# Odd attention of a two-block diffusion model on one core: one activation for both sinks, and one turned tile in four copied by VectorE

## The chip, the core and the metric

The kernel runs on one core of a Trainium2 chip. The metric is the device time of one execution in microseconds. The kernel before took 2181.8 us, the median of 3 runs (2180.72 to 2182.32).

## What is computed

The reference is two transformer blocks in fp32, one after the other, on 256 tokens of width 1024 (`first_block` and `second_block`). The change touches only the attention of the second block's odd layer, `window_attention`: 16 query heads in groups of four on 4 key heads of width 64, 256 latent tokens that see the latent keys at a distance of at most 128 and all 256 context keys, and one sink logit a head that takes part in the softmax and has no value:

```python
s_loc = einsum(q, k) * scale            # banded: |i-j| <= 128, else -inf
s_ctx = einsum(q, k_c) * scale
m = max(max(s_loc), max(s_ctx), s_sink)
e_loc, e_ctx = exp(s_loc - m), exp(s_ctx - m)
denom = sum(e_loc) + sum(e_ctx) + exp(s_sink - m)
o = (e_loc @ v + e_ctx @ v_c) / denom
```

## The kernel before, in words

Every engine has its own program, written out by hand, and engines wait for each other's named events: `done` adds to an engine's output semaphore and books the event's name, and the other side waits for the count at that name. `link` makes an engine wait for its own last instruction before it goes on, and `own` for an earlier event of its own. The weights come in 1 MB chunks through a ring of three buffers. ScalarE makes the high part of each chunk (L1519, `whi`) and VectorE the rest (L2056, `wlo`), and TensorE multiplies both parts (L629 to L631, or L635 and L639 in the feed-forward phases). The phases follow each other; the odd layer (`odd` in each engine's program) lies between the MLP phase M0 and the last MLP phase M1.

The odd attention has 16 steps `s`. Step `s` treats the two query heads (`e` = 0, 1) of pair `p = s // 2` for one half of the queries, 128 of them (`qt = s % 2`). The 512 keys (256 latent, 256 context) are the columns of a PSUM bank. `R` is banks 0 to 3 and `Y` is banks 4 to 7 of `banks`. Buffers that depend on `s % 2` come twice. What happens to step `s`:

- TensorE, `scores(s)`: q x k of both heads into two banks of `R` (L1404), and the window's mask added by a matmul (L1407).
- VectorE, `maxima(s)`: the row maximum of both heads in one reduction of 1024 columns (L2824), then the negative maximum with the sink taken in, `stat[o + 2:o + 4]` (L2826), event `odmax`.
- ScalarE, `exps(s)`: the exponentials with row sums (L1954, twice), then the exponential of each sink (L1957, twice), event `odexp`. This event also frees the two banks of `R` for `scores(s + 2)`.
- VectorE, `normalise(s)`: sums (L2832), reciprocal (L2833), the two products (L2835, twice), event `odprob`.
- TensorE, `turn(s)`: eight 128x128 transposes (L903), four of head 0 into bank `Y[:, 2]` and four of head 1 into `Y[:, 3]`, with one event each, `odpt`. Each bank must have been emptied of step `s - 1`.
- ScalarE, `take(s)`: one 128x512 copy a head out of these banks into `pt` (L1966).
- TensorE, `values(s)`: the probabilities times the values (L1429), event `odpv`; after an odd `s` ScalarE's `take_o` (L1971) takes the pair's result.

The order that each engine goes through is written out as a loop: TensorE `scores(s + 2)`, four products of the last query chunk if `s < 4`, `turn(s)`, `values(s - 1)`, and at `s = 5` the rotation's matmuls `rot(5)` (L1365). VectorE `maxima(s + 1)`, `normalise(s)`, in steps 2 and 3 half a weight chunk (L2056), and at `s = 6` `rotate(5)`, the rotary embedding of the last query heads (L2583 to L2585). ScalarE `exps(s + 1)`, `take(s)`, and `take_o` in even steps from 2 on. Before the loop VectorE does `maxima(0)` and `rotate(4)`. Behind it the kernel casts the attention's result (L1988, L2258) and multiplies it with the output weights (`odo`).

Of the kernel before, what the change touches and what calls it, by code (L numbers as in the profile page):

```python
# [19 lines left out]
ALU = mybir.AluOpType  # L20
ACT = mybir.ActivationFunctionType
AX_X = mybir.AxisListType.X

P = 128
# [97 lines left out]
def program(nc, A, out_ap, book):  # L122
    ctx = ExitStack()
    with ctx:
# [97 lines left out]
        def ec(name, k=0, n=None):  # L222
            a, w = ecol_at[name]
            return ecol[:, a + k:a + k + (w - k if n is None else n)]
# [389 lines left out]
        def _(pe):  # L614
# [732 lines left out]
            def odd():  # L1347
# [62 lines left out]
                def turn(s):  # L1410
                    pe.wait_ge(dve_out.sem, dve_out.at(("odprob", s)))
                    for e in range(2):
                        if s >= 1:
                            pe.wait_ge(drained.sem, drained.at(("odpt", s - 1, e)))
                        for kt in range(4):
                            last = transpose(Y[:, 2 + e, kt * P:(kt + 1) * P], O["p"][s % 2][:, e, kt * P:(kt + 1) * P])
                        last.then_inc(pe_out.sem, pe_out.next(("odpt", s, e)))

                def values(s):
                    p, qt = s // 2, s % 2  # L1420
                    pe.wait_ge(drained.sem, drained.at(("odpt", s, 1)))
                    if qt == 0 and p == 0:
                        pe.wait_ge(dve_out.sem, dve_out.at(("odrope", 4)))
                    if qt == 0 and p >= 1:
                        pe.wait_ge(drained.sem, drained.at(("odo", p - 1)))
                    at = (p % 2) * T + qt * P
                    for kt in range(4):
                        for e in range(2):
                            last = mm(Y[64 * e:64 * e + 64, 0, at:at + P], O["vtok"][:, kt, 64 * (p // 2):64 * (p // 2) + 64],  # L1429
                                      O["pt"][s % 2][:, kt, e * P:(e + 1) * P], start=kt == 0, stop=kt == 3, skip_group_check=True)  # L1430
                    last.then_inc(pe_out.sem, pe_out.next(("odpv", s)))
# [64 lines left out]
        def _(act):  # L1496
# [10 lines left out]
            def done(ins, key):  # L1507
                ins.then_inc(act_out.sem, act_out.next(key))
# [405 lines left out]
            def odd():  # L1914
# [35 lines left out]
                def exps(s):  # L1950
                    o = 20 * (s % 2)
                    act.wait_ge(dve_out.sem, dve_out.at(("odmax", s)))
                    for e in range(2):
                        f(O["p"][s % 2][:, e, :], R[:, 2 * (s % 2) + e, :], ACT.Exp, scale=SCALE,  # L1954
                          bias=stat[:, o + 2 + e:o + 3 + e], accum_out=stat[:, o + 6 + e:o + 7 + e])
                    for e in range(2):
                        last = f(stat[:, o + 8 + e:o + 9 + e], ec("sink", 2 * (s // 2) + e, 1), ACT.Exp, scale=-1.0,  # L1957
                                 bias=stat[:, o + 2 + e:o + 3 + e])
                    done(last, ("odexp", s))

                def take(s):
                    for e in range(2):
                        act.wait_ge(pe_out.sem, pe_out.at(("odpt", s, e)))
                        if s >= 2 and e == 0:
                            act.wait_ge(pe_out.sem, pe_out.at(("odpv", s - 2)))
                        nc.scalar.copy(O["pt"][s % 2][:, :, e * P:(e + 1) * P], Y[:, 2 + e, :].rearrange("p (a q) -> p a q", a=4)) \  # L1966
                            .then_inc(drained.sem, drained.next(("odpt", s, e)))
# [65 lines left out]
        def _(dve):  # L2033
# [9 lines left out]
            def done(ins, key):  # L2043
                ins.then_inc(dve_out.sem, dve_out.next(key))

            def own(key):
                dve.wait_ge(dve_out.sem, dve_out.at(key))
# [738 lines left out]
            def odd():  # L2786
# [32 lines left out]
                def maxima(s):  # L2819
                    o = 20 * (s % 2)  # L2820
                    p, qt = s // 2, s % 2
                    dve.wait_ge(pe_out.sem, pe_out.at(("ods", s)))
                    scores = R[:, 2 * (s % 2):2 * (s % 2) + 2, :]
                    link(v.tensor_reduce(stat[:, o:o + 2], scores, AX_X, ALU.max))  # L2824

                    done(v.scalar_tensor_tensor(out=stat[:, o + 2:o + 4], in0=stat[:, o:o + 2], scalar=-SCALE, in1=ec("sink", 2 * p, 2),  # L2826
                                                op0=ALU.mult, op1=ALU.min), ("odmax", s))

                def normalise(s):
                    o = 20 * (s % 2)  # L2830
# [4 lines left out]
                        last = v.tensor_scalar(O["p"][s % 2][:, e, :], O["p"][s % 2][:, e, :], stat[:, o + 12 + e:o + 13 + e], None, ALU.mult)  # L2835
                    done(last, ("odprob", s))

                maxima(0)
                rotate(4)
                for s in range(16):  # L2840
                    if s + 1 < 16:
                        maxima(s + 1)
                    normalise(s)
                    if s in (2, 3):
                        conv(n + 7, (s - 2,))
                    if s == 6:
                        rotate(5)
                split_lo("odo", src=O["q"])
                alpha(resx)
                n = first["odo"]  # L2850
# [116 lines left out]
```

## Time and profile before

| what | value |
|---|---|
| median of 3 runs | 2181.8 us |
| lowest and highest | 2180.72, 2182.32 us |
| profiled execution, its own time | 2183.51 us |
| profiled execution, span | 2181.7 us, 33428 instructions |
| TensorE, VectorE, ScalarE busy | 97%, 81%, 54% of the span |
| HBM traffic | 503.29 MB read, 231 GB/s over the span |
| the odd attention's 16 steps | about 1888 to 1952 us |

The span is the time from the first to the last instruction on the core; the execution's own time is 1.8 us more. Busy time counts an engine's instructions alone, without waits, branches and DMA issues. The durations below are those of this one execution.

### The profile page before, as it was taken

Reading aid. Unit: us, or ns where it says so; the run is one execution under the profiler, and the core shown is the slowest. Engines: PE = TensorE matmul, PEld = TensorE weight load, DVE = VectorE, ACT = ScalarE, POOL = GpSimd, SP = SyncE. Lnnn points to the kernel's source line nnn. Section 1 sums busy time; section 2 is a strip of 40 time slices with the busy share of each in tenths; the row PEclk is TensorE's granted clock in tenths of the full one; section 3 lists DMA queues with packets and bytes.
Section 4 is the critical chain, followed back from the end, with each engine's and each line's share of the span. In section 5 each row is a group of like instructions: output and inputs, shape, how many; then the busy total and the mean of one; then the engine's idle time right before and its main releaser. Section 6 shows DMA issues by size and latency. Waiting matters only on the chain.

```text
span 2181.7 us, 33428 instructions
## 1 busy us (share of the span) xinstructions
PE 2120.3 (97%) x13811; PEld 1857.7 (85%) x13820; DVE 1777.2 (81%) x2350; ACT 1175.9 (54%) x1759; POOL 109.5 (5%) x157
## 2 busy tenths in 40 slices
PE   7999999999999999999999999999999999999997
PEld 4888888888888888898888989988888888778886
DVE  4888787788878878977888877898998998777764
ACT  3555556555455445565553544547646744575742
POOL 1000000000000000000000000000000000000000
PEclk9999999999999999999999999999999999999999
DMA  9889675478868877655888747738878877315662
GB/s 331 288 274 317 219 245 193 155 252 282 312 196 276 281 272 234 228 188 171 278 276 286 235 161 223 244 126 291 281 268 292 295 255 248 117 35 160 212 212 78
DMA packets 331024, 506.51 MB, mean 232 GB/s; under 512 B 12392, under 2 KB 239943, under 8 KB 330872
## 3 DMA queue, kind: packets, MB, share of 16 engines
q1 hardware_dynamic: 288647, 342.01, 47.7%
q0 software_dynamic: 41616, 160.44, 21.3%
q8 instruction: 109, 1.79, 0.3%
q10 hardware_dynamic: 608, 1.92, 0.3%
q14 instruction: 44, 0.35, 0.0%
HBM read 503.29 MB, written 1.05 MB: 231 GB/s over the span
## 4 chain that ended last, share of the span: by engine, by line
PE 89%; DVE 7%; DMA 2%; ACT 1%; issue 1%; POOL 0%; DVEq 0%; POOLq 0%
PE banks L635 38%; PE banks L639 19%; PE banks L629 7%; PE banks L631 6%; PE banks L630 6%; DMA plain_xs<-in_ada_w_dram 1%; PE banks L841 1%; PE banks L903 1%; PE banks L736 1%; PE banks L738 1%; PE banks L737 1%; DVE wlo L2056 1%; PE banks L1404 1%; DVE nraw L2334 1%; DMA stage<-in_ffn_wg_dram 1%
## 5 line engine op out<-in xcount | busy, mean ns | idle before, releaser
L2056 DVE TENSOR_TENSOR wlo<-stage,whi 128x1024 fp32r<-128x1024 f32 x644 | 758.3, 1219 | 124.4 <-ACT whi L1519 123.3
L1519 ACT CAST whi<-stage 128x1024 fp32r<-128x1024 f32 x644 | 643.8, 1052 | 336.5 <-PE banks L639 257.9
L635 PE MATMUL banks<-xs,whi 128*128 128x512 f32 x2176 | 688.1, 398 | 13.6 <-DVE xs L2338 9.5
L639 PEld LDWEIGHTS banks<-xs,wlo 128*128 128x128 f32 x2176 | 409.9, 188 | 97.0
L639 PE MATMUL banks<-xs,wlo 128*128 128x256 f32 x2176 | 428.6, 278 | 0.0
L629 PE MATMUL banks<-xs,whi 128*128 128x256 f32 x1216 | 351.1, 289 | 10.4 <-DVE xs L2338 5.6
L635 PEld LDWEIGHTS banks<-xs,whi 128*128 128x128 f32 x2176 | 332.2, 189 | 18.7 <-DVE xs L2338 7.6
L630 PE MATMUL banks<-xs,whi 128*128 128x256 f32 x1216 | 343.9, 283 | 0.0
L631 PE MATMUL banks<-xs,wlo 128*128 128x256 f32 x1216 | 343.9, 283 | 0.0
L635 PE MATMUL banks<-hidden_arena,whi 128*128 128x512 f32 x992 | 311.8, 395 | 0.0
L2081 DVE SCALAR_TENSOR_TENSOR arena<-modw,cact,arena 128x1024 f32<-128x1024 f32 x217 | 277.9, 1280 | 10.5 <-DMA modw<-in_w_mod_dram 6.7
L629 PEld LDWEIGHTS banks<-xs,whi 128*128 128x128 f32 x1216 | 232.9, 192 | 20.5 <-issue 8.9
L630 PEld LDWEIGHTS banks<-xs,whi 128*128 128x128 f32 x1216 | 233.0, 192 | 0.6 <-issue 0.2
L631 PEld LDWEIGHTS banks<-xs,wlo 128*128 128x128 f32 x1216 | 233.0, 192 | 0.0
L639 PEld LDWEIGHTS banks<-hidden_arena,wlo 128*128 128x128 f32 x992 | 186.5, 188 | 42.6
L639 PE MATMUL banks<-hidden_arena,wlo 128*128 128x256 f32 x992 | 195.8, 279 | 0.0
L635 PEld LDWEIGHTS banks<-hidden_arena,whi 128*128 128x128 f32 x992 | 150.1, 188 | 0.4
L610 POOL DMA_DIRECT2D modw<-in_w_mod_dram x80 | 57.1, 714 | 1125.8 <-DVE arena L2081 944.4
L635 PE MATMUL banks<-hs,whi 128*128 128x512 f32 x336 | 105.6, 395 | 0.3 <-issue 0.3
L1539 ACT COPY hid<-banks 128x512 f32<-128x512 f32 x44 | 26.0, 590 | 112.9 <-PE banks L639 112.9
L610 POOL DMA_DIRECT2D modw<-in_ada_w_dram x64 | 45.7, 714 | 753.6 <-DVE arena L2081 668.6
L1535 ACT COPY hid<-banks 128x512 f32<-128x512 f32 x44 | 26.0, 590 | 105.6 <-PE banks L639 105.6
(442 smaller groups left out, 2620.7 us busy)
## 6 DMA issues: line engine op xcount, KB each, us to landing
stage<-in_mlp_w_dram SPq DMA_DIRECT2D x96, 1024.0 KB, 5.4
modw<-in_w_mod_dram POOLq DMA_DIRECT2D x80, 1024.0 KB, 6.0
modw<-in_ada_w_dram POOLq DMA_DIRECT2D x66, 1024.0 KB, 5.5
stage<-in_ffn_wg_dram SPq DMA_DIRECT2D x44, 1024.0 KB, 5.5
stage<-in_ffn_wu_dram SPq DMA_DIRECT2D x44, 1024.0 KB, 7.4
stage<-in_ffn_wd_dram SPq DMA_DIRECT2D x44, 1024.0 KB, 7.4
stage<-in_ev_w_in_dram SPq DMA_DIRECT2D x24, 1024.0 KB, 5.9
stage<-in_w_in_dram SPq DMA_DIRECT2D x18, 1024.0 KB, 5.4
```

The source lines that it names most:

```text
L610: pool.dma_start(modw[:, c % 2, :].rearrange("p (a b) -> p a b", a=2), src).then_inc(mod_landed[c % 2], 16)
L629: mm(out, hi, xh, start=first_mm, stop=False, skip_group_check=True)
L630: mm(out, hi, xl, start=False, stop=False, skip_group_check=True)
L631: return mm(out, lo, xh, start=False, stop=last_mm, skip_group_check=True)
L635: return mm(out, whi[:, s, w:w + P], pair.rearrange("p a t -> p (a t)"), start=first_mm, stop=False, skip_group_check=True)
L639: return mm(out[:, 0:T], wlo[:, s, w:w + P], pair[:, 0, :], start=False, stop=last_mm, skip_group_check=True)
L736: mm(out, xh, hi, start=k == 0, stop=False, skip_group_check=True)
L1519: nc.scalar.copy(halves(whi[:, s, :], n, h, True), halves(stage[:, s, :], n, h)).then_inc(hi_done, 1)
L1535: done(nc.scalar.copy(hid[:, j % 2, :, :], R[:, 0:2, T:2 * T]), ("gate", name, j))
L1539: done(nc.scalar.copy(hid[:, 2, :, :], R[:, 2:4, T:2 * T]), ("up", name, j - 1))
L2056: last = v.tensor_tensor(halves(wlo[:, s, :], n, h, True), halves(stage[:, s, :], n, h), halves(whi[:, s, :], n, h, True).bitcast(F32), AL ...
L2081: v.scalar_tensor_tensor(out=acc, in0=w, scalar=cc, in1=acc, op0=ALU.mult, op1=ALU.add).then_inc(mod_step, 1)
```

## The change

Three things are altered, in the odd attention alone.

1. VectorE computes the sinks' shifted exponents itself: after `maxima` it waits for its own `odmax` and subtracts the stored sinks from the negative maxima (2 columns, `stat[o + 14:o + 16]`), event `odsink`. ScalarE waits for it and takes one exponential of both columns in place of two of one column each.
2. In odd steps ScalarE's `take` copies only head 0's turned tile. VectorE copies head 1's in `take_second(s)`, which stands between `maxima` and `normalise` of the step that follows, and after the loop for step 15. It signals on a semaphore of its own, `drained_v`.
3. TensorE waits for that semaphore where the tile of an odd step is read (`values`) or overwritten (`turn`). ScalarE in odd steps from 3 on waits for the turn of two steps before, since it no longer takes that step's last tile itself.

```diff
--- before.py
+++ after.py
@@ -1410,7 +1410,9 @@
                 def turn(s):
                     pe.wait_ge(dve_out.sem, dve_out.at(("odprob", s)))
                     for e in range(2):
-                        if s >= 1:
+                        if s >= 1 and e == 1 and s % 2 == 0:
+                            pe.wait_ge(drained_v.sem, drained_v.at(("odpt", s - 1, 1)))
+                        elif s >= 1:
                             pe.wait_ge(drained.sem, drained.at(("odpt", s - 1, e)))
                         for kt in range(4):
                             last = transpose(Y[:, 2 + e, kt * P:(kt + 1) * P], O["p"][s % 2][:, e, kt * P:(kt + 1) * P])
@@ -1418,7 +1420,11 @@
 
                 def values(s):
                     p, qt = s // 2, s % 2
-                    pe.wait_ge(drained.sem, drained.at(("odpt", s, 1)))
+                    if qt == 0:
+                        pe.wait_ge(drained.sem, drained.at(("odpt", s, 1)))
+                    else:
+                        pe.wait_ge(drained.sem, drained.at(("odpt", s, 0)))
+                        pe.wait_ge(drained_v.sem, drained_v.at(("odpt", s, 1)))
                     if qt == 0 and p == 0:
                         pe.wait_ge(dve_out.sem, dve_out.at(("odrope", 4)))
                     if qt == 0 and p >= 1:
@@ -1950,16 +1956,16 @@
                 def exps(s):
                     o = 20 * (s % 2)
                     act.wait_ge(dve_out.sem, dve_out.at(("odmax", s)))
+                    if s >= 2 and s % 2 == 1:
+                        act.wait_ge(pe_out.sem, pe_out.at(("odpt", s - 2, 1)))
                     for e in range(2):
                         f(O["p"][s % 2][:, e, :], R[:, 2 * (s % 2) + e, :], ACT.Exp, scale=SCALE,
                           bias=stat[:, o + 2 + e:o + 3 + e], accum_out=stat[:, o + 6 + e:o + 7 + e])
-                    for e in range(2):
-                        last = f(stat[:, o + 8 + e:o + 9 + e], ec("sink", 2 * (s // 2) + e, 1), ACT.Exp, scale=-1.0,
-                                 bias=stat[:, o + 2 + e:o + 3 + e])
-                    done(last, ("odexp", s))
+                    act.wait_ge(dve_out.sem, dve_out.at(("odsink", s)))
+                    done(f(stat[:, o + 8:o + 10], stat[:, o + 14:o + 16], ACT.Exp), ("odexp", s))
 
                 def take(s):
-                    for e in range(2):
+                    for e in range(2 - s % 2):
                         act.wait_ge(pe_out.sem, pe_out.at(("odpt", s, e)))
                         if s >= 2 and e == 0:
                             act.wait_ge(pe_out.sem, pe_out.at(("odpv", s - 2)))
@@ -2825,6 +2831,8 @@
 
                     done(v.scalar_tensor_tensor(out=stat[:, o + 2:o + 4], in0=stat[:, o:o + 2], scalar=-SCALE, in1=ec("sink", 2 * p, 2),
                                                 op0=ALU.mult, op1=ALU.min), ("odmax", s))
+                    own(("odmax", s))
+                    done(v.tensor_tensor(stat[:, o + 14:o + 16], stat[:, o + 2:o + 4], ec("sink", 2 * p, 2), ALU.subtract), ("odsink", s))
 
                 def normalise(s):
                     o = 20 * (s % 2)
@@ -2835,16 +2843,26 @@
                         last = v.tensor_scalar(O["p"][s % 2][:, e, :], O["p"][s % 2][:, e, :], stat[:, o + 12 + e:o + 13 + e], None, ALU.mult)
                     done(last, ("odprob", s))
 
+                def take_second(s):
+                    dve.wait_ge(pe_out.sem, pe_out.at(("odpt", s, 1)))
+                    if s >= 2:
+                        dve.wait_ge(pe_out.sem, pe_out.at(("odpv", s - 2)))
+                    v.tensor_copy(O["pt"][s % 2][:, :, P:2 * P], Y[:, 3, :].rearrange("p (a q) -> p a q", a=4)) \
+                        .then_inc(drained_v.sem, drained_v.next(("odpt", s, 1)))
+
                 maxima(0)
                 rotate(4)
                 for s in range(16):
                     if s + 1 < 16:
                         maxima(s + 1)
+                    if s >= 1 and s % 2 == 0:
+                        take_second(s - 1)
                     normalise(s)
                     if s in (2, 3):
                         conv(n + 7, (s - 2,))
                     if s == 6:
                         rotate(5)
+                take_second(15)
                 split_lo("odo", src=O["q"])
                 alpha(resx)
                 n = first["odo"]
```

TensorE's instructions stand in the same order as before; only its waits differ. On VectorE, this is one step of the loop before, from `maxima(s + 1)` to the end of `normalise(s)` (`ecol` is the room of `stat`, `banks` is PSUM, `arena` holds the probabilities; the words in brackets are the semaphores that a row waits for):

```order
L2824 TENSOR_REDUCE ecol<-banks 128x2 [waits pe_out]
L2826 SCALAR_TENSOR_TENSOR ecol<-ecol 128x2 [waits dve_chain]
L2832 TENSOR_TENSOR ecol<-ecol 128x2 [waits act_out]
L2833 RECIPROCAL ecol<-ecol 128x2 [waits dve_chain]
L2835 TENSOR_SCALAR arena<-arena,ecol 128x512 [waits dve_chain]
L2835 TENSOR_SCALAR arena<-arena,ecol 128x512
```

And this is an even step of the loop now, from 2 on (lines below the edit are moved by it):

```order
L2830 TENSOR_REDUCE ecol<-banks 128x2 [waits pe_out]
L2832 SCALAR_TENSOR_TENSOR ecol<-ecol 128x2 [waits dve_chain]
L2835 TENSOR_TENSOR ecol<-ecol 128x2 [waits dve_out]
L2850 COPY arena<-banks 128x4x128 [waits pe_out]
L2840 TENSOR_TENSOR ecol<-ecol 128x2 [waits act_out]
L2841 RECIPROCAL ecol<-ecol 128x2 [waits dve_chain]
L2843 TENSOR_SCALAR arena<-arena,ecol 128x512 [waits dve_chain]
L2843 TENSOR_SCALAR arena<-arena,ecol 128x512
```

The small subtraction (L2835) has come into every step behind the small row that it waits for, and the copy (L2850) into every even step, ahead of the rows of `normalise`. An odd step is the same without the copy.

On ScalarE, this is an even step and the start of the odd one behind it, before: `exps`, `take` (two copies), `take_o`, `exps`, `take`:

```order
L1954 ACTIVATE arena,ecol<-banks,ecol 128x512 [waits dve_out]
L1954 ACTIVATE arena,ecol<-banks,ecol 128x512
L1957 ACTIVATE ecol<-ecol 128x1 x2
L1966 COPY arena<-banks 128x4x128 [waits pe_out] x2
L1971 COPY arena<-banks 128x256 [waits pe_out]
L1954 ACTIVATE arena,ecol<-banks,ecol 128x512 [waits dve_out]
L1954 ACTIVATE arena,ecol<-banks,ecol 128x512
L1957 ACTIVATE ecol<-ecol 128x1 x2
L1966 COPY arena<-banks 128x4x128 [waits pe_out] x2
```

And the same place now:

```order
L1962 ACTIVATE arena,ecol<-banks,ecol 128x512 [waits pe_out,dve_out]
L1962 ACTIVATE arena,ecol<-banks,ecol 128x512
L1965 ACTIVATE ecol<-ecol 128x2 [waits dve_out]
L1972 COPY arena<-banks 128x4x128 [waits pe_out] x2
L1977 COPY arena<-banks 128x256 [waits pe_out]
L1962 ACTIVATE arena,ecol<-banks,ecol 128x512 [waits dve_out]
L1962 ACTIVATE arena,ecol<-banks,ecol 128x512
L1965 ACTIVATE ecol<-ecol 128x2 [waits dve_out]
L1972 COPY arena<-banks 128x4x128 [waits pe_out]
```

Each pair of sink exponentials (L1957) has become one with a wait for VectorE (L1965), and the second `take` here, that of an odd step, has one copy instead of two.

## Rows read from the trace of the kernel before

**Rows 1.** The page's first table: busy us, share of the span, instructions.
```profile
PE 2120.3 (97%) x13811; PEld 1857.7 (85%) x13820; DVE 1777.2 (81%) x2350; ACT 1175.9 (54%) x1759; POOL 109.5 (5%) x157
```

**Rows 2.** Stretches: us, PE, PEld, DVE, ACT, POOL busy, clock, DMA share, GB/s.
```profile
1896.20:1912.95 16.75, 16.75 (x140) 12.54 (x141) 12.23 (x26) 13.89 (x39) 0.00 (x0) 1.00 0.20 64
1912.97:1944.30 31.33, 31.33 (x274) 20.65 (x274) 24.43 (x57) 26.25 (x76) 0.00 (x0) 1.00 0.01 2
...
1954.15:2181.70 227.55, 212.23 (x1271) 186.07 (x1272) 154.79 (x196) 117.66 (x158) 1.43 (x2) 0.98 0.49 162
```

**Rows 3.** Timeline of PE, turn 11 to turn 12: start, us, what.
```profile
1937.60 1.06 PE L903 MATMUL banks<-base,arena 128*128 128x128 f32 x8
1938.59 1.09 PE L1429 MATMUL banks<-arena 128*64 128x128 f32 x16
1939.62 1.13 PE L1404 MATMUL banks<-arena 64*128 64x512 f32 x4
...
1940.95 1.06 PE L903 MATMUL banks<-base,arena 128*128 128x128 f32 x8
```

**Rows 4.** Timeline of ACT, steps 11 and 12; brackets: idle before, its releaser.
```profile
1937.99 0.48 ACT L1957 ACTIVATE ecol<-ecol 128x1 f32<-128x1 f32 x2
1938.36 1.07 ACT L1966 COPY arena<-banks 128x512 f32<-128x512 f32 x2
...
1941.61 1.07 ACT L1966 COPY arena<-banks 128x512 f32<-128x512 f32 x2 [0.47 <-PE banks L903]
1943.08 0.37 ACT L1971 COPY arena<-banks 128x256 f32<-128x256 f32 x1 [0.40 <-PE banks L1429]
```

**Rows 5.** Timeline of DVE, its step 13: maxima(14) and normalise(13).
```profile
1941.15 1.22 DVE L2824 TENSOR_REDUCE ecol<-banks 128x2 f32<-128x1024 f32 x1 [0.74 <-PE banks L1407]
1942.41 0.16 DVE L2826 SCALAR_TENSOR_TENSOR ecol<-ecol 128x2 f32<-128x2 f32 x1
1942.49 0.15 DVE L2832 TENSOR_TENSOR ecol<-ecol 128x2 f32<-128x2 f32 x1
1942.67 0.17 DVE L2833 RECIPROCAL ecol<-ecol 128x2 f32<-128x2 f32 x1
1942.88 0.88 DVE L2835 TENSOR_SCALAR arena<-arena,ecol 128x512 f32<-128x512 f32 x2
```

**Rows 6.** Timelines of PE and DVE at the start: scores(2), turn(0), normalise(0).
```profile
1893.01 1.13 PE L1404 MATMUL banks<-arena 64*128 64x512 f32 x4 [1.52 <-ACT ecol L1957]
...
1896.19 1.09 PE L903 MATMUL banks<-base,arena 128*128 128x128 f32 x8 [0.20 <-DVE arena L2835]
...
1895.25 0.88 DVE L2835 TENSOR_SCALAR arena<-arena,ecol 128x512 f32<-128x512 f32 x2
```

**Rows 7.** Timelines of DVE and PE: normalise(6), rotate(5), normalise(7), turn(7).
```profile
1918.25 0.88 DVE L2835 TENSOR_SCALAR arena<-arena,ecol 128x512 f32<-128x512 f32 x2
1919.57 0.69 DVE L2583 TENSOR_TENSOR hid<-banks,table 128x512 f32<-128x512 f32 x1 [0.44 <-PE banks L1365]
...
1923.22 0.88 DVE L2835 TENSOR_SCALAR arena<-arena,ecol 128x512 f32<-128x512 f32 x2
...
1924.16 1.09 PE L903 MATMUL banks<-base,arena 128*128 128x128 f32 x8
```

**Rows 8.** Timeline of PE, turn(14) and its wait.
```profile
1947.17 1.09 PE L903 MATMUL banks<-base,arena 128*128 128x128 f32 x8 [0.78 <-DVE arena L2835]
```

**Rows 9.** Groups by shape: line, engine, operation, out<-in, count, busy us, mean ns, idle.
```profile
L2583 DVE TENSOR_TENSOR hid<-banks,table 128x512 f32<-128x512 f32 x5 | 3.4, 688 | 6.0 <-PE banks L1365 6.0
L2835 DVE TENSOR_SCALAR arena<-arena,ecol 128x512 f32<-128x512 f32 x32 | 14.1, 484 | 0.6
L2274 DVE TENSOR_SCALAR hid<-banks 128x256 f32<-128x256 f32 x5 | 2.1, 425 | 6.3 <-ACT hid L1618 6.3
L2266 DVE SCALAR_TENSOR_TENSOR arena<-banks,arena 128x256 f32<-128x256 f32 x3 | 1.3, 424 | 0.1
L2426 DVE COPY pcol<-banks 128x392 f32<-128x392 f32 x1 | 0.9, 852 | 0.0
```

## Prediction

> **What bounds the kernel now.** I read the page's first table, then the table of stretches with its granted clock, then the timeline of each engine inside the odd attention, then the chain of waits. The page says that TensorE (PE) is busy for 97% of the span, VectorE (DVE) for 81%, ScalarE (ACT) for 54% [rows 1]. A share over the whole span does not say who sets the pace of this stage, so the stretches matter. From 1912.97 to 1944.30 us, nine of the sixteen steps and the rotation of the last queries, PE is busy 31.33 of 31.33 us at a clock of 1.00, ACT 26.25 and DVE 24.43 [rows 2]. ACT is the busier helper, but PE never waits for it.
>
> The timeline of PE shows one step: turn 0.99, values 1.03, scores and window masks 1.33, then the next turn, 3.35 us in all, with no bracket of idle time on any row [rows 3]. Step 12 to 13 lasts as long, from 1940.95 to the stretch's end at 1944.30, where turn 13 starts. ACT waits for PE in it: 0.47 before `take`, 0.40 before `take_o` [rows 4]. `take_o` runs in even steps alone, and still even and odd steps last 3.35 us alike, so ACT's extra 0.37 + 0.40 us is not on the path.
>
> DVE is nearer to it. In its step 13 `maxima` starts 0.20 after PE has started turn 12 (1941.15 against 1940.95), and the last probability is normalised at 1942.88 + 0.88 = 1943.76, 2.61 us later [rows 3, 5]. PE follows DVE by 0.06 where it does wait (1895.25 + 0.88 = 1896.13, then 1896.19) [rows 6]. So DVE's way from one turn to the next is 0.20 + 2.61 + 0.06 = 2.87 of 3.35 us: **0.48 us of slack a step**. At three places it has none. Turn 0 waits for `normalise(0)` [rows 6]. Turn 7 starts at 1924.16, 0.06 after DVE's 1923.22 + 0.88 = 1924.10, because `rotate(5)` stands in front of it on DVE [rows 7]. And turn 14 waits 0.78 us: PE has no scores left to compute in this step, and the chain of waits, PE's own for nearly all of the stage, passes through DVE here [rows 8]. Behind the stage PE is busy 212.23 of 227.55 us and the chain stays on it [rows 2], so a shift of the stage's end is a shift of the kernel's end.
>
> **ScalarE's side of the change: nothing.** Two sink exponentials take 1938.36 - 1937.99 = 0.37 us of ACT's queue, and one takes half, so 0.185 goes in each of 16 steps. One of two copies goes in each of 8 odd steps, half of 1.07 [rows 4]. This is 3.0 + 4.3 = 7.2 us of ACT's time, and it all turns into longer waits for PE. The exponentials' end also releases `scores(s + 2)`. At step 0 PE did idle 1.52 us there, but behind it PE waited again for DVE before turn 0 [rows 6]; the earlier scores make only that second wait longer. The new wait for the sink on ACT stands behind two exponentials of 0.7 us each, and the sink is ready 0.35 us after `odmax`: free. So is ACT's new wait for the turn two steps back.
>
> **VectorE's side: two additions.** The sink's shift comes 16 times. It is a 2-column subtraction that must wait for the row before it. Without such a wait the next small row follows after 0.08 us (1942.41 to 1942.49), with one after 0.18 to 0.19 (1942.49 to 1942.67) [rows 5]. The shift waits and what follows doesn't, so it puts **0.19 us** on DVE's way. A page speaks against this number: the Trainium skill's "VectorE: DVE Perf Modes", section "The DRAIN you can't avoid", says that a semaphore after each of eight Vector copies cost nothing extra. Were that so here, the shift would cost 0.08, and the sum below would be 1.54 instead of 2.28. The rows decide for 0.19.
>
> The copy of 128x512 out of PSUM comes 8 times, in even steps before `normalise`, and after step 15. No such copy is in the trace. The nearest row is L2583, a 128x512 read of the banks with a second input, 0.69 us busy; less the 0.08 by which a row without a wait overlaps the one before it (0.16 busy, 0.08 from start to start) that is 0.61 [rows 5, 9]. I take **0.61 us**, because a 128x256 one-input operation out of the banks, 0.425, equals a two-input one's 0.424, so one input gives nothing. The lower end is a 128x512 operation within SBUF, 0.484 - 0.08 = 0.40 [rows 9]. The upper end is the only copy out of the banks, 0.852 for 392 columns in a strided order, or 0.852 x 512 / 392 = 1.11 [rows 9].
>
> An odd step has 2.87 + 0.19 = 3.06 against 3.35: hidden. An even step has 2.87 + 0.19 + 0.61 = **3.67 against 3.35: 0.32 us late**. DVE, on time again in the odd step behind it, gives nothing back: PE paces that one. Now in order:
> - Turn 0: +0.19 (the shift of step 1 stands before `normalise(0)`).
> - Turns 1 to 6: nothing. Up to step 3 four query products lie in each PE step, and step 5 has the rotation's matmuls; from 1896.20 to 1912.95 DVE is busy 12.23 of 16.75 us, 4.5 spare in four steps, for two copies and four shifts that want 2.0 [rows 2].
> - Turn 7: `normalise(6)` ended at 1919.13 and `rotate(5)` began at 1919.57. It now ends 0.80 later, at 1919.93, and the rotation starts at 1919.95, 0.38 later. With the shift of step 8 turn 7 is 0.38 + 0.19 = 0.57 late.
> - Turn 8: DVE comes straight from turn 7's probabilities here, 0.04 before PE starts to turn them, and 2.61 + 0.80 + 0.06 - 0.04 = 3.43 against 3.35: +0.08.
> - Turns 10 and 12: 2 x 0.32 = 0.64.
> - Turn 14, with no slack: 0.19 + 0.61 = +0.80.
> - Turn 15 and the end: PE has to do turn 14 and values 13 first, 2.1 us, in which DVE's 1.3 us of `normalise(15)` fit. The last copy waits for turn 15 and lies beside values 14.
>
> The sum is 0.19 + 0.57 + 0.08 + 0.64 + 0.80 = **+2.28 us**. Against the profiled execution's own 2183.51 us that is 2185.8; this execution lies 1.7 above the median of the three runs, 2181.8, so the forecast for a median is **2184.1**. That is +0.10%, within the 0.2% (4.4 us) that a measurement of this kernel can tell from no change.
>
> **The bounds.** With a copy of 0.40 and a shift of 0.08 the even step needs 3.35: nothing is lost at turns 8, 10 and 12, and 0.08 + 0.14 + 0.48 = +0.7 us is left (2182.5). With a copy of 1.11 turns 7, 8, 10, 12 and 14 pay it, and the sum is 2.28 + 5 x 0.5 = 4.8 us, 5.0 with the 0.2 that turn 4 may add where its spare time runs out (2186.8).
>
> **The rivals.**
> - *ScalarE sets the pace after all.* If PE's unbroken rows hid waits for ACT's copies, the whole 7.2 us would be gained: 2174.6, -0.3%. For it: ACT's 26.25 us are the most of the helpers. Against it: equal odd and even steps, and ACT waiting 0.87 us for PE in each pair. Chance 0.04.
> - *The copy on VectorE is dear, and the kernel is slower.* The place is `take_second` in even steps, ahead of `normalise` on DVE; PE waits for it at turns 8, 10, 12 and 14. From a copy of 1.0 us on the total passes 4.4 us (each 0.1 us above 0.61 costs about 0.5 us); at 1.11 it is 5.0 us, 2186.8 or more, +0.23%. For it: the one copy of this kind ran at 2.2 ns a column. Against it: that one is strided, this one has rows of 128 columns. Chance 0.09.
> - *VectorE's slack covers it.* The copy is as short as its lower end, or DVE's 0.20 of late start vanishes, and only the start, turn 7 and turn 14 pay: +0.7 to +1.0 us, 2182.5 to 2182.8. For it: 0.48 us of slack. Against: the row that I took. Chance 0.25.
> - *The change doesn't do what it says.* The instruction lists show it done on both engines, so no chance of its own.
>
> **How the numbers follow.** The forecast's case holds 0.62. Only the first rival is faster by over 0.2% (0.04), only the second is slower (0.09), the rest, 0.87, is within it. The range goes down from the lower end's 2182.5 by the scatter of the runs (1.1 us below the median) and a little more to 2181.0, and up to the dear copy's 2186.8, rounded to 2187.0.
>
> **What would show it.** In the new profile: `take_second`'s copies at 0.69 us busy; DVE's row after the shift 0.19 later; ACT's idle before `take` longer by some 0.2 to 0.7 us; PE rows of turns 8, 10 and 12 with idle time of 0.05 and 0.3 us that `normalise` ends, and turn 14 waiting some 1.6 us instead of 0.78; steps lasting 3.35 and 3.67 in turn. I am wrong if even and odd steps stay equal (slack held), if the step gets shorter than 3.35 (ACT was the pace), or if the stage's clock falls below 1.00, which no row of it does now.

## The result, and the profile after

The changed kernel took **2185.62 us**, the median of 22 runs (2181.68 to 2190.34); the kernel before took 2182.23 us on the same chip, 22 runs (2178.64 to 2187.47). The ratio is 1.0016 [1.0010, 1.0023]: 3.5 us slower, between 2.2 and 5.0. The forecast was 2184.1 us in a range of 2181.0 to 2187.0, and 2.28 us of added work. That the change costs a little and stays within 0.2% came true; the median is 1.5 us above the forecast.

The page's first table of the changed kernel answers to [rows 1]:

```profile
PE 2122.2 (97%) x13811; PEld 1859.2 (85%) x13820; DVE 1783.4 (82%) x2374; ACT 1168.2 (54%) x1735; POOL 109.5 (5%) x157
```

VectorE has 24 instructions more (16 shifts, 8 copies) and 6.2 us more of work, ScalarE 24 fewer and 7.7 us less. The span is 2183.2 us, the execution's own time 2185.11.

The same three stretches of time as in [rows 2]. They do not hold the same instructions: the changed kernel reached the stage 3.7 us sooner in this execution, about one step (columns: us, PE, PEld, DVE, ACT, POOL busy, clock, DMA share, GB/s):

```profile
1896.20:1912.95 16.75, 16.75 (x150) 12.36 (x149) 13.30 (x32) 11.21 (x27) 0.00 (x0) 1.00 0.21 65
1912.97:1944.30 31.33, 30.43 (x267) 20.06 (x265) 27.37 (x67) 22.22 (x64) 0.00 (x0) 1.00 0.01 2
...
1954.15:2183.00 228.85, 214.48 (x1263) 188.01 (x1263) 153.26 (x194) 116.19 (x156) 1.43 (x2) 0.96 0.49 161
```

In the second, PE is no longer unbroken: it idles 0.90 us (0.68 before turns 7, 10 and 12, and the first 0.22 of its wait before turn 14, which lay outside this stretch in [rows 2]), DVE does 2.9 us more and ACT 4.0 less. In the last the clock reads 0.96 where it was 0.98.

The timeline of PE in the changed kernel, turns 7, 8, 10, 11, 12, 13 and 14. It answers to [rows 3, 7, 8]:

```profile
1921.16 1.09 PE L903 MATMUL banks<-base,arena 128*128 128x128 f32 x8 [0.38 <-DVE arena L2843]
...
1924.54 1.06 PE L903 MATMUL banks<-base,arena 128*128 128x128 f32 x8
...
1931.56 1.09 PE L903 MATMUL banks<-base,arena 128*128 128x128 f32 x8 [0.15 <-DVE arena L2843]
...
1934.94 1.06 PE L903 MATMUL banks<-base,arena 128*128 128x128 f32 x8
...
1938.61 1.09 PE L903 MATMUL banks<-base,arena 128*128 128x128 f32 x8 [0.15 <-DVE arena L2843]
...
1941.99 1.06 PE L903 MATMUL banks<-base,arena 128*128 128x128 f32 x8
...
1945.66 1.09 PE L903 MATMUL banks<-base,arena 128*128 128x128 f32 x8 [1.58 <-DVE arena L2843]
```

Every bracket is a wait for the probabilities that `normalise` (now L2843) leaves, and they stand before turns 7, 10, 12 and 14. Turns 8, 9, 11 and 13 have none. No row of any engine waits for the copy (L2850) itself, so the trace shows no cost of TensorE's new semaphore; the copy counts only because `normalise` stands behind it. Turn 12 comes 3.67 us after turn 11 (1938.61 - 1934.94) and turn 13 3.38 after turn 12: the steps of 3.67 and 3.35 that were forecast, with 0.03 us more behind a wait. The bracket shows only half of this delay: a turn that need not wait starts before the recorded end of the row ahead of it (turn 12 of [rows 3] 0.16 before: the mask's matmuls ahead of it ran from 1940.67 for 0.44 us), and that overlap is lost too when it waits. So **starts are to be subtracted, not brackets added up**.

DVE in an even step, maxima(13), the new shift (L2835), the new copy (L2850), normalise(12), which answers to [rows 5]:

```profile
1935.14 1.22 DVE L2830 TENSOR_REDUCE ecol<-banks 128x2 f32<-128x1024 f32 x1 [0.89 <-PE banks L1407]
1936.40 0.16 DVE L2832 SCALAR_TENSOR_TENSOR ecol<-ecol 128x2 f32<-128x2 f32 x1
1936.60 0.16 DVE L2835 TENSOR_TENSOR ecol<-ecol 128x2 f32<-128x2 f32 x1
1936.68 0.69 DVE L2850 COPY arena<-banks 128x512 f32<-128x512 f32 x1
1937.28 0.15 DVE L2840 TENSOR_TENSOR ecol<-ecol 128x2 f32<-128x2 f32 x1
1937.47 0.17 DVE L2841 RECIPROCAL ecol<-ecol 128x2 f32<-128x2 f32 x1
1937.67 0.88 DVE L2843 TENSOR_SCALAR arena<-arena,ecol 128x512 f32<-128x512 f32 x2
```

The shift starts 0.20 after the row it waits for, and the copy follows it by 0.08 (0.19 were forecast for the addition). The copy takes 0.69 us busy and 0.60 from start to start (0.61). From the start of `maxima` to that of the products there are 2.53 us, where [rows 5] have 1.73: +0.80, as forecast.

ACT from exps(13) to take_o(12), which answers to [rows 4]:

```profile
1937.94 0.20 ACT L1965 ACTIVATE ecol<-ecol 128x2 f32<-128x2 f32 x1
1939.30 1.07 ACT L1972 COPY arena<-banks 128x512 f32<-128x512 f32 x2 [1.17 <-PE banks L903]
1940.77 0.37 ACT L1977 COPY arena<-banks 128x256 f32<-128x256 f32 x1 [0.40 <-PE banks L1435]
```

The sinks' exponential is 0.20 us where two took 0.48, and what ACT saves it waits: 1.17 us before `take(12)` instead of 0.47. Over the whole stage ACT's waits for turned tiles rose from 5.5 to 12.9 us in the waits views. All its waits together rose by 9.5 us (5.7 to 7.2 for the maxima, 4.0 to 4.6 for the values): the 7.2 that the forecast counts as freed, and the 2.2 by which the stage is longer.

### A measure that chance does not reach

Runs of one kernel scatter by 9 us, more than any term here. The stage is steadier: from the first row of `scores(1)` (L1404) to the first row of `odo` (L629) it took 65.07, 65.07 and 65.06 us in the three profiles of the kernel before, and 67.27, 67.29 and 67.28 in the three of the changed one. The change costs **2.20 us** there. This is how it grows, from the starts of turns in the two first profiles:

| place | forecast | measured |
|---|---|---|
| turn 0 | +0.19 | +0.19 |
| turns 1 to 6 | 0 | 0.00 to +0.01 |
| turn 7 | +0.57 | +0.47 |
| turn 8 | +0.08 | 0.00 |
| turn 10 | +0.32 | +0.31 |
| turn 12 | +0.32 | +0.35 |
| turn 14 | +0.80 | +0.83 |
| turn 15 to `odo` | 0 | +0.05 |
| sum | +2.28 | +2.20 |

Turns 9, 11 and 13, which the table leaves out, are counted with the turn behind them; 0.03 us of turn 12's 0.35 and of turn 14's 0.83 arise already at turns 11 and 13.

The medians show 3.5 [2.2, 5.0]. So 1.3 us is left over, near the edge of what they can tell. Both kernels were measured twice more as they are (below), each time with 11 runs of the changed kernel and 44 of the one before. The three differences of the mean times are 3.4, 2.4 and 3.8 us, together 3.1 [2.5, 3.8]. So the stage's 2.20 us alone is too little, and some 0.9 us [0.3, 1.6] lies elsewhere. A place for it is in the profile too, right behind the stage: the first six microseconds of `odo`, first in the kernel before, then in the changed one:

```profile
1954.15:1960.15 6.00, 6.00 (x50) 6.00 (x51) 5.15 (x6) 3.97 (x5) 0.00 (x0) 1.00 0.01 3
```

```profile
1952.69:1958.69 6.00, 6.00 (x38) 6.00 (x39) 5.16 (x6) 3.98 (x5) 0.00 (x0) 0.72 0.01 3
```

TensorE is busy throughout in both, but at a granted clock of 0.72 it gets through 38 matmuls instead of 50. At full clock they follow each other by 0.12 us, so 12 of them are about 1.4 us. In the timeline the distance between matmuls is 0.21 us from 1953.4 on for some 3.4 us, the lower of the clock's two levels (1.2 GHz instead of 2.4), and before it PE had waited 1.93 us for the cast of the attention's result. That wait is just as long in the kernel before (1.94 us).

### The profile page after: what moved, and what is told of

Read it like the earlier page. It is cut to its first block, busy times and chain, and to the rows that moved or that the text cites. A ratio compares the mean times of both kernels' runs of the same rounds, so it can differ in the third digit from the quotient of the medians.

```text
span 2183.2 us, 33450 instructions
## 1 busy us (share of the span) xinstructions
PE 2122.2 (97%) x13811; PEld 1859.2 (85%) x13820; DVE 1783.4 (82%) x2374; ACT 1168.2 (54%) x1735; POOL 109.5 (5%) x157
## 4 chain that ended last, share of the span: by engine, by line
PE 88%; DVE 7%; DMA 2%; ACT 1%; issue 1%; POOL 0%; DVEq 0%; POOLq 0%
PE banks L635 38%; PE banks L639 19%; PE banks L629 6%; PE banks L631 6%; PE banks L630 6%; DMA plain_xs<-in_ada_w_dram 1%; PE banks L841 1%; PE banks L903 1%; PE banks L736 1%; PE banks L738 1%; PE banks L737 1%; DVE wlo L2062 1%; DVE nraw L2340 1%; DMA stage<-in_ffn_wg_dram 1%; DVE arena L2087 1%
## 5 line engine op out<-in xcount | busy, mean ns | idle before, releaser
L629 PE MATMUL banks<-xs,whi 128*128 128x256 f32 x1216 | 351.8, 289 | 10.4 <-DVE xs L2344 5.3
L629 PEld LDWEIGHTS banks<-xs,whi 128*128 128x128 f32 x1216 | 233.6, 192 | 20.5 <-issue 8.8
```

Source lines behind the costliest of these rows:

```text
L629: mm(out, hi, xh, start=first_mm, stop=False, skip_group_check=True)
```

## The experiments

The theory: every microsecond comes by VectorE's way to the next turn, 0.20 us for each shift and 0.60 for each copy, where that way is longer than PE's step. The rivals: the new waits on ScalarE or TensorE's new semaphore cost the time; and, for what the stage does not explain, the clock. All kernels below compute the whole layer. "Stage" is the measure above; each ratio is against the kernel before in runs on the same chip.

### Each half alone

The sinks alone, on the kernel before (nothing is done to the copies):

```diff
-                    for e in range(2):
-                        last = f(stat[:, o + 8 + e:o + 9 + e], ec("sink", ...), ACT.Exp, scale=-1.0, bias=...)
-                    done(last, ("odexp", s))
+                    act.wait_ge(dve_out.sem, dve_out.at(("odsink", s)))
+                    done(f(stat[:, o + 8:o + 10], stat[:, o + 14:o + 16], ACT.Exp), ("odexp", s))
...
+                    own(("odmax", s))
+                    done(v.tensor_tensor(stat[:, o + 14:o + 16], ..., ALU.subtract), ("odsink", s))
```

> Only the sinks' part of the change: one exponential of two columns on shifted biases; all copies stay on ScalarE. Measure: the stage, from the start of scores(1) to the first row of the odo phase, is 65.07 us in the kernel before and 67.27 in the changed one. If VectorE's way to the turns is what counts (my theory), the shift costs 0.19 us at turns 0, 7 and 14 and nothing elsewhere: a stage of 65.6 us, the kernel 0.6 us slower. If ScalarE sets the pace (rival), 16 x 0.185 us go: 62 us. Second question, the clock: if the longer wait of turn 14 brings the clock down in odo, this kernel with 0.97 us of wait there instead of 0.78 should keep 1.00 nearly as often as the kernel before.

2184.31 us, ratio 1.0004 [0.9995, 1.0013]; stage 66.00 us, +0.93. Turn 0 is 0.19 late and turn 14 another 0.19, as each should be. Turn 7 is 0.55 late, and 0.19 were due. The cause is in one gap, PE's rotation matmuls and VectorE's row that reads them:

```profile
1918.82 1.12 PE L1365 MATMUL banks<-arena,base 128*128 128x512 f32 x2
...
1920.40 0.69 DVE L2581 TENSOR_TENSOR hid<-banks,table 128x512 f32<-128x512 f32 x1 [0.59 <-PE banks L1365]
```

From start to start there are 1.58 us. In the profiles of the kernel before, with filled waits or without, there are 1.23 to 1.24, as here in the first one (1919.57 in [rows 7]):

```profile
1918.34 1.12 PE L1365 MATMUL banks<-arena,base 128*128 128x512 f32 x2
```

The kernel with the sinks alone was therefore run again:

> The sinks' part alone once more. Its stage was 66.0 us where 65.6 was expected: the rotation of the last queries began 1.58 us after TensorE's rotation matmuls had started, against 1.23 to 1.24 in both profiles of the kernel before, though VectorE was idle 0.59 us. If that is fixed by the order of the program, the stage is 66.0 again; if it was a chance of that one execution, it is 65.6.

2183.53 us, 1.0010 [1.0001, 1.0019]; stage 65.99, and the gap is 1.58 again. So it belongs to the program and not to chance. Why 0.35 us are added there is open. In the changed kernel VectorE comes to this row 1.51 us after the matmuls' start, straight from its work and without idle time, so there nothing of this gap shows.

The copies alone, on the changed kernel:

```diff
-                    act.wait_ge(dve_out.sem, dve_out.at(("odsink", s)))
-                    done(f(stat[:, o + 8:o + 10], stat[:, o + 14:o + 16], ACT.Exp), ("odexp", s))
+                    for e in range(2):
+                        last = f(stat[:, o + 8 + e:o + 9 + e], ec("sink", ...), ACT.Exp, scale=-1.0, bias=...)
+                    done(last, ("odexp", s))
...
-                    own(("odmax", s))
-                    done(v.tensor_tensor(stat[:, o + 14:o + 16], ..., ALU.subtract), ("odsink", s))
```

> Only the copies' part: VectorE copies the second turned tile of odd steps, the sinks stay on ScalarE. By my theory, an even step needs 2.87 + 0.61 = 3.48 us on VectorE against TensorE's 3.35: 0.13 each at turns 10 and 12, some 0.1 at turn 7, 0.61 at turn 14: a stage of 66.0 us, 0.9 us over the kernel before. If ScalarE sets the pace (rival), 8 x 0.5 us go: 61 us. If the parts add up, this and the other part make 1.5 of the 2.2 us; the rest, 0.7, is what the slack of 0.48 us absorbs for each alone.

2184.49 us, 1.0004 [0.9996, 1.0013]; stage 66.11 us, +1.04: 0.07 at turn 7, 0.12 to 0.13 at turns 10 and 12, and all of the copy at turn 14.

```profile
1944.60 1.09 PE L903 MATMUL banks<-base,arena 128*128 128x128 f32 x8 [1.39 <-DVE arena L2843]
```

The wait is 1.39 us where it was 0.78 [rows 8], +0.61 for one copy. An even step that has the copy alone needs 2.87 + 0.61 = 3.48 against 3.35 us, and 0.12 to 0.13 of it comes through: the slack of 0.48 is real, and the size of the copy too. The other 0.11 us of the 1.04 are 0.03 each at turns 11 and 13 and 0.05 between turn 15 and `odo`. The halves do not add up to the whole at turns 10 and 12 (0.31 and 0.35 against 0 and 0.12 to 0.13), since the slack is spent once.

### Where there is no slack: the last even step

The changed kernel, but step 13's second tile copied by ScalarE:

```diff
-                        if s >= 1 and e == 1 and s % 2 == 0:
+                        if s >= 1 and e == 1 and s % 2 == 0 and s != 14:
...
-                    if qt == 0:
+                    if qt == 0 or s == 13:
...
-                    for e in range(2 - s % 2):
+                    for e in range(2 if s == 13 else 2 - s % 2):
...
-                    if s >= 1 and s % 2 == 0:
+                    if s >= 1 and s % 2 == 0 and s != 14:
```

> The changed kernel with one copy taken back to ScalarE: that of step 13, which stood on VectorE before turn 14's probabilities, where the chain of waits ran through VectorE. If a term of my sum is right, turn 14 waits 0.97 us instead of 1.58 and the stage falls from 67.28 to 66.7 us. Clock: the fall at the start of odo was in both profiles of the changed kernel (idle 1.58 and 1.93 us within 10 us before it) and in none of the four others (idle up to 1.39 and 1.93). If TensorE's idle time brings it about (theory), it is gone here, and the kernel is 0.6 + 1.5 = 2.1 us faster than the changed one. If it is chance (rival), it is here or not, whatever the wait.

2184.07 us, 1.0010 [1.0000, 1.0019]; stage 66.67 us, 0.60 less than the changed kernel.

```profile
1946.19 1.09 PE L903 MATMUL banks<-base,arena 128*128 128x128 f32 x8 [0.97 <-DVE arena L2843]
```

Turn 14 waits 0.97 = 0.78 + 0.19 us: the shift alone is left. This takes a copy back from VectorE and gives it to ScalarE, and only gains. So ScalarE's extra work and its waits are not the cause, and the copy's price is counted a second time at 0.61 us. `odo` starts at a clock of 1.00 here.

### The clock in `odo`

Is the low clock behind the stage the change's doing, and is it the longer wait at turn 14 that brings it? First more profiles of both kernels as they are:

> The changed kernel once more, for its profile: a stage of 67.3 us with TensorE idle 0.38 before turn 7, 0.15 before turns 10 and 12, 1.58 before turn 14, as the schedule fixes these. In the first profile the granted clock fell to half for 3.4 us at the start of odo and again at the start of M1. If the change brings that about (theory), it is there again. If it is chance (rival), it is there or not, as in the kernel before.

> The kernel before once more, for its profile: a stage of 65.1 us. The granted clock at the start of odo and of M1 stayed at 1.00 in its first profile. If the change alone brings the falls about, it does so again; if they are chance, one may show here. The time is that of the kernel before: ratio 1.000 within 0.1%.

2185.29 us, 1.0011 [1.0002, 1.0019], and 2183.28 us, 1.0005 [0.9996, 1.0013]. `odo` starts at 0.72 again in the changed kernel and at 1.00 in the one before. Now waits are filled, one in each kernel, with matmuls of zeros into a free bank (`keep_warm`). In the changed kernel, turn 14's wait:

```diff
+                    if s == 14:
+                        keep_warm(Y[:, 1, :], 6)
```

> The changed kernel with six matmuls on zeros (0.22 us each, 1.3 us) before turn 14, in its wait of 1.58 us; nothing waits for them. The stage stays 67.3 us. If the idle time before turn 14 is what brings the clock down in odo (theory), the clock stays at 1.00 there and the kernel gains up to 1.5 us on the changed one. If the fall has another cause (rival), it shows as before.

2185.23 us, 1.0017 [1.0008, 1.0026]; stage 67.29. In this profile PE has work up to turn 14 and waits there for 0.16 us only, and `odo` is slow all the same:

```profile
1948.93 1.25 PE L704 MATMUL banks<-base 128*128 128x512 bf16 x5 [0.16 <-issue]
1950.35 1.09 PE L903 MATMUL banks<-base,arena 128*128 128x128 f32 x8 [0.16 <-DVE arena L2845]
...
1957.39 0.35 PE L629 MATMUL banks<-xs,whi 128*128 128x256 f32 x1 [1.93 <-DVE xs L2266]
```

```profile
1957.39:1963.39 6.00, 6.00 (x38) 6.00 (x39) 5.16 (x6) 3.97 (x5) 0.00 (x0) 0.72 0.01 3
```

So the fall does not need turn 14's wait. Then the 1.93 us before `odo`, in either kernel:

```diff
+                keep_warm(R[:, 3, :], 8)
                 first_chunk(n, Y[:, 0, :], "odo")
```

> The changed kernel with eight matmuls on zeros (1.75 us) in the wait of 1.93 us before the first row of odo. The stage stays 67.3 us, or up to 0.1 longer if they end late. Theory: the clock in odo stays at 1.00, up to 1.5 us faster than the changed kernel. Rival: the fall shows all the same, or comes elsewhere.

> The kernel before with the same eight matmuls on zeros before odo: a candidate to beat both. Its profiles held 1.00 in odo without them, so by the theory nothing is gained there: ratio 1.000 within 0.1%, a stage of 65.1 us. If the kernel before also loses clock at this place in some of its runs (rival), the mean gain is some part of 1.5 us, up to 0.07%.

The changed kernel with it: 2183.27 us, 1.0005 [0.9996, 1.0014], stage 67.27, and `odo`'s first microseconds are at 1.00:

```profile
1953.88:1959.88 6.00, 6.00 (x50) 6.00 (x51) 5.15 (x6) 3.98 (x5) 0.00 (x0) 1.00 0.01 3
```

The kernel before with it: 2182.67 us, 1.0002 [0.9993, 1.0011], stage 65.06, clock 1.00, as without. On one chip, then, the changed kernel was 1.0017 with turn 14's wait filled and 1.0005 with `odo`'s wait filled, a difference in the direction of the clock's 1.5 us; these intervals overlap. Set directly against each other, the two versions' 11 runs differ by 2.0 us in the medians and by 2.7 [1.3, 4.2] in the means, and their mean granted clocks are 0.9955 and 0.9967. That fits a gain of 1.5 us by the fill before `odo`; the two versions differ in the fill at turn 14 as well, and the changed kernel without any fill was not run on this chip.

A third profile of each kernel spoils the simple story:

> The changed kernel a third time, for its profile: stage 67.3 us. The fall of the clock at the start of odo was in both profiles of it and in the one with turn 14's wait filled, and in none of the five of kernels with a shorter stage and the same wait of 1.93 us before odo. If it belongs to the changed kernel, it is here; if it was chance at 3 in 8, it is here in 4 cases of 10. On average over runs the changed kernel then loses up to 1.5 us more than its stage.

> The kernel before a third time, for its profile: stage 65.1 us, clock 1.00 at the start of odo if the fall belongs to the changed kernel.

2186.84 us, 1.0019 [1.0010, 1.0028], and 2182.94 us, 1.0003 [0.9994, 1.0012]. The stage is as ever (67.28, 65.06), but in the kernel **before** `odo` starts slow this time, too:

```profile
1954.96:1960.96 6.00, 6.00 (x37) 6.00 (x38) 5.16 (x6) 3.97 (x5) 0.00 (x0) 0.72 0.01 3
```

All profiles taken, by the clock in `odo`'s first six microseconds:

| kernels | at 0.72 | at 1.00 |
|---|---|---|
| changed, wait before `odo` as it is (turn 14's wait filled in one) | 4 | 0 |
| before, the sinks alone, the copies alone, step 13's copy back | 1 | 6 |
| wait before `odo` filled (changed once, before twice) | 0 | 3 |

The fall is no property of the changed kernel alone. It comes more often there, as far as 4 of 4 and 1 of 7 can say (4 of 5 and 1 of 6 if step 13's copy back, one copy away from the changed kernel, is counted with it). Why the same wait of 1.93 us is followed by it in one execution and not in another is open.

What the falls cost can be read from the same profiles, because the span is the sum of three parts: up to the stage, the stage, and from `odo` to the end. In us:

| profile | up to the stage | stage | from `odo` on | clock below 1.00 at the start of |
|---|---|---|---|---|
| before, first | 1889.08 | 65.07 | 227.55 | neither |
| before, second | 1886.54 | 65.07 | 228.79 | M1 |
| before, third | 1889.90 | 65.06 | 229.04 | `odo` |
| changed, first | 1885.42 | 67.27 | 230.51 | `odo` and M1 |
| changed, second | 1887.83 | 67.29 | 229.08 | `odo` |
| changed, third | 1885.15 | 67.28 | 229.07 | `odo` |

The fall in `odo` costs 1.5 us to the very end, one at M1's start 1.2 to 1.4 (0.8 to 0.9 in the profiles where the clock fell for a shorter time there). But the two places partly stand in for each other: of the 5 profiles with the fall in `odo` 1 has one at M1, and of the 6 with neither place filled and `odo` at 1.00, 5 have one at M1. So `odo` alone overstates what the clock costs the changed kernel: its last part is longer by 1.1 us on average over three profiles each (229.55 against 228.46), and 2.2 + 1.1 = 3.3. The granted clock of every run points the same way but not evenly: its mean is 0.9956 over the 44 runs of the changed kernel and 0.9960 over 121 of the kernel before, which is 0.9 us of the span [0.2, 1.6]; taken apart, that is 0.0 us in the runs with the second profiles and 1.3 in those with the third.

### A version that might beat both

The kernel before with three waits filled: before `odo`, at the end of the odd layer and in front of M1.

```diff
+                    if k == 2 and key == "M1":
+                        keep_warm(R[:, 3, :], 5)
...
+                keep_warm(R[:, 3, :], 8)
...
-                keep_warm(R[:, 3, :], 16)
+                keep_warm(R[:, 3, :], 21)
```

> The kernel before with zeros' matmuls in every wait of 1 us or more around the end of the stage: eight before odo, and at the start of M1 five more in front of its first row and five before its third block of rows. The clock at the start of M1 fell to half for about 3.4 us in 6 of the 10 profiles so far, of whichever kernel. If TensorE's waits there bring it about (theory), it holds 1.00 in odo and in M1, and the kernel is up to 1 us faster on average than before, 0.05%; too little to be told by the times, so the profile decides. If not (rival), the fall shows all the same.

2181.38 us, ratio 0.9994 [0.9986, 1.0003], stage 65.04: not to be told from no change. The clock did what it should, shown here 30 us after the start of `odo`, first in the second profile of the kernel before, then in this version:

```profile
1981.61:1996.61 15.00, 12.56 (x54) 10.27 (x54) 12.74 (x24) 8.77 (x15) 0.00 (x0) 0.77 0.22 68
```

```profile
1982.25:1997.25 15.00, 13.59 (x70) 10.08 (x69) 13.37 (x24) 9.79 (x16) 0.00 (x0) 1.00 0.22 71
```

The place at M1's start was slow in 7 of the 13 profiles of all kernels that were not filled there, so a fill can win there only part of what one fall costs. From `odo` on this version took 227.55 us, just what the first profile of the kernel before took, which has no fall there. No run found a version that is surely faster than the kernel before.

## Why the prediction was right, and where it was not

- **What bounds the stage.** Right. PE sets a step of 3.35 us and VectorE has 0.48 us of slack; the copies alone (0.12 to 0.13 us late of 0.61) show that size directly.
- **ScalarE's side at nothing.** Right: its 7.2 us turned into longer waits (9.5 us with the 2.2 of the longer stage). `scores(2)` comes 0.28 us sooner (its wait is 1.24 instead of 1.52 us), and turn 0 waits 0.67 instead of 0.20, as foreseen. The rival in which ScalarE is the pace is out: it wanted 7.2 us less, and the stage grew by 2.20.
- **The shift at 0.19, the copy at 0.61.** Right: 0.20 and 0.60. The rule of the Trainium skill, "VectorE: DVE Perf Modes", section "The DRAIN you can't avoid", by which the semaphore costs nothing extra, would have made the shift 0.08 and the sum 1.54. The trace disagrees for rows this small: in all 16 steps the shift starts 0.19 to 0.20 us after the row that it waits for, and a row behind the shift that need not wait starts 0.07 to 0.08 after it. The dear copy of 1.11 is out with this, and so is the copy of 0.40.
- **Turn 7 at +0.57.** Mis-sized: +0.47. The step that failed said that `rotate(5)` starts 0.02 behind the end of `normalise(6)`. The row without a wait starts before the one in front has ended, here 0.08 us before:

```profile
1915.59 0.88 DVE L2843 TENSOR_SCALAR arena<-arena,ecol 128x512 f32<-128x512 f32 x2
1916.39 0.68 DVE L2589 TENSOR_TENSOR hid<-banks,table 128x512 f32<-128x512 f32 x1
```

  1915.59 + 0.88 = 1916.47 against 1916.39. I had used this overlap for the copy and forgotten it here.
- **Turn 8 at +0.08.** Measured 0.00, by the same forgotten overlap. `maxima(9)` starts 0.13 us before turn 7 (1921.16) and not 0.04, so DVE's way is 2.61 + 0.80 + 0.06 - 0.13 = 3.34 us, and PE's step behind a wait is 3.38:

```profile
1921.03 1.21 DVE L2830 TENSOR_REDUCE ecol<-banks 128x2 f32<-128x1024 f32 x1
```

- **Turns 10, 12, 14: 0.32, 0.32, 0.80.** Right: 0.31, 0.35, 0.83. The sign named for them, idle time of 0.3 us, was not: the brackets say 0.15, since a wait also takes away an overlap that no bracket shows.
- **The end at nothing.** +0.05 us there. The last two groups of values, between turn 15 and the end, take longer by about that (2.04 us as the trace groups them, 1.97 before). It belongs to the copies: from turn 15 to `odo` there are 4.99 us with them, 5.00 with them alone, and 4.93 with the sinks alone, as in the kernel before.
- **From the stage's end to the kernel's.** This step was incomplete. I took the stage's shift for the kernel's, and thought of a clock below 1.00 only in the stage, where it stayed at 1.00. The part behind the stage was 1.1 us longer in the changed kernel on average over three profiles each, by falls of the clock in `odo` and at M1's start, and that is about what the times show beyond the stage's 2.20. That the falls come with the change, and not by chance in these few profiles, is not shown. That the median came out 1.5 us above the forecast and still inside the range is in this respect luck: the range was made for the copy's price and the scatter.
- **The base.** One profiled execution is a poor zero. The two first profiles differ by only 1.5 us in span: the one before had lost 3.7 us more ahead of the stage, where among others its clock was 0.90 from 40 to 60 us and 0.93 from 60 to 80 (1.00 and 1.00 in the changed one). Then come +2.20 in the stage and, by the falls in `odo` and at M1's start, 230.51 - 227.55 = 3.0 behind it: -3.7 + 2.2 + 3.0 = 1.5.

## What to carry to other kernels

Work that is moved off an engine which waits is worth nothing, and where it goes it is paid as far as it exceeds that engine's slack per step: so measure the slack (here 0.48 us a step, and none where PE has nothing left to do) before the move. Compare the starts of the same instructions in both traces over the stage that was edited; that told 0.02 us here, where medians of 22 runs told 1.4. And look at the granted clock on both sides of the edit before a difference of spans is put down to it.

## What the runs showed of the chip that I had not expected

- A wait of 1.93 us on TensorE was followed by some 3.4 us at half clock (0.72 over six microseconds, about 1.5 us lost) in 5 of 11 profiles, and in 0 of 3 where matmuls of zeros filled it. What decides between them is open. Where it fell there, the next place, at M1's start, mostly kept its clock (4 of 5), and where it did not, M1's start mostly fell (5 of 6).
- One and the same program can gain or lose some microseconds by such falls in places that an edit never touches: 0.90 and 0.93 against 1.00 between 40 and 80 us of the two first profiles.
- A VectorE row waited 1.58 us from the start of the matmuls it reads in one program, twice, and 1.23 to 1.24 in the kernel before, which differs around it by the sinks alone. No cause was found.
